# Out projection of a transformer block as three products of rounded halves, with the second norm computed row tile by row tile inside it

## Chip, cores, metric

One Trainium2 chip, one of its eight cores. The metric is device time in microseconds (us) of one execution; the median of the runs is compared.

## What is computed

Two transformer blocks follow each other on 256 tokens of 1024 channels, all in float32. The change lies at the end of the first block's mixer and in the norm behind it:

```
cat = concatenate([fourier(f), o_att, dn], axis=-1)      # 256 + 512 + 256 channels
x = x + g1 * (cat @ w_out)                               # w_out 1024 x 1024
h2 = rms(x, norm2) * (1 + sc2) + sh2                     # x*rsqrt(mean(x*x)+eps)*norm2
x = x + g2 * (square(relu(h2 @ w_ff1)) @ w_ff2)          # w_ff1 1024x4096, w_ff2 4096x1024
```

`dn` is the output of a gated delta rule in four heads, itself rms-normed per head and multiplied by a silu gate.

## The kernel before

Each engine has its own instruction stream, written by hand; the engines meet at semaphores. Tokens are in two row tiles t of 128, output channels in two halves hh of 512, contracted channels in eight groups k of 128. A list of jobs (`first_jobs`) gives every PSUM product a number, a bank and the engine that empties it; `w.open(name)` on TensorE waits until the bank's old job is emptied, `w.after(name)` until that job itself is, `r.open(name)` on a reader waits until the job is full. Banks 0 to 3 hold the four sums (t, hh) of the out projection.

Before the change, attention and the scan of the delta rule run in eight steps n; ScalarE copies transposed probabilities (`PT`), takes exponentials, and scales the products (`PV`). Behind step 7:

- TensorE transposes the attention output (`catA0`, `catA1`, line 2237), waits for `dn_ready`, transposes `dn` (`catD`, 2243), spreads the gate vectors g1 and g2 over all rows (`g0_*`, `g1_*`, line 2251, eight matmuls each, two records a matmul), and forms the out projection in float32 (line 2259, 32 matmuls of 512 columns, two records each). Eight matmuls on constants (`dense`, line 616) and a wait for `hat_ready` follow, then 16 transposes of the normed rows (`h2T0` to `h2T3`, 2269), `mlp_open` (line 693, four matmuls that open banks 0 to 3), and the MLP's loop (716, 718, 729).
- VectorE sums `dn` (2820, 2821), scales it with a factor that GpSimd raises to the power -0.5 (`power(5, ...)`, lines 2516 and 2519), and counts `dn_ready`. Then `add_gated(0)`: for each (t, hh) two instructions (2833, 2836) as the sum fills (`acc_full`); `split_low` (755); scale and shift of the transposed norm (2856); `split_y` (785).
- ScalarE copies the products out (2298), rounds the first MLP weights (`split_high`, 747), squares the two rows tile by tile (2486), waits for GpSimd's `power(6, ...)`, scales the rows (2493), and rounds the shifted channels (`y_high`, 2498).

The MLP already multiplies in halves: a number is the sum of a rounded part (high, a copy into the type fp32r on ScalarE) and the rest (low, a subtraction on VectorE), and a product is high*high + high*low + low*high. Weights come through a ring of four slots of 2 MB; `out0` and `out1` lie in slots 0 and 1, and the loads into these slots wait for `acc_full` 3 and 4. TensorE enters the MLP when `y_split` is 2 and `w_low` is 4.

## Time and profile before

| | us |
|---|---|
| three runs | 1560.35, 1561.5, 1569.91 (median 1561.5) |
| profiled execution, its own time | 1570.09 |
| its span, first to last instruction | 1568.3 |
| mean granted TensorE clock | 0.967 |

The profiled execution is 8.6 us above the median, and 1.8 us of its time lie outside its span. Times in the rows below are us from the span's start.

### The profile page before, as it was taken

To read this page: it belongs to the slowest core of one execution; us is meant where nothing else is said; L and a number is where in the kernel's file an instruction comes from. 1 tells how busy PE (TensorE), PEld (TensorE's weight loads), DVE (VectorE), ACT (ScalarE), POOL (GpSimd) and SP (SyncE) were. 2 spreads that over 40 slices of the span, in tenths; PEclk is the share of its full clock that TensorE was granted. 3 is DMA by queue.
4 is the path that set the end of the run, shared out by engine and by line. 5 is a ranking of instruction groups with operands and counts; after the bars stand their busy time and mean duration, and the time that the engine had idled before them with its cause. 6 is when DMAs were issued, how large, how long until landed. Compare 5 with 4: busy or idle time off the path is not lost. (4 is left out here: it accounts for less than half of the span.)

```text
span 1568.3 us, 25730 instructions
## 1 busy us (share of the span) xinstructions
PE 1472.4 (94%) x10597; PEld 1198.7 (76%) x10597; DVE 903.9 (58%) x1410; ACT 695.0 (44%) x1168; POOL 58.3 (4%) x73
## 2 busy tenths in 40 slices
PE   5999989988999989999899999998999989999996
PEld 2556767655888879898877888878989887788885
DVE  1653343425656556377586655575657768565655
ACT  3232325433444434376732444453547653344442
POOL 0000530000000000000000000000000000000000
PEclk9999999988999999999999999999999989999998
DMA  9630651006554426433237555524534223846420
GB/s 349 257 108 17 236 185 53 2 1 215 180 192 166 134 82 187 141 108 108 108 108 264 184 195 189 186 82 141 163 109 144 89 89 108 305 177 214 179 89 27
DMA packets 121038, 230.14 MB, mean 147 GB/s; under 512 B 20080, under 2 KB 34672, under 8 KB 120176
## 3 DMA queue, kind: packets, MB, share of 16 engines
q1 hardware_dynamic: 118064, 223.80, 41.0%
q10 hardware_dynamic: 2880, 5.01, 0.9%
q8 instruction: 68, 1.11, 0.3%
q14 instruction: 26, 0.21, 0.0%
HBM read 227.76 MB, written 1.05 MB: 146 GB/s over the span
## 5 line engine op out<-in xcount | busy, mean ns | idle before, releaser
L755 DVE TENSOR_TENSOR work_rounded<-ring,work_rounded 128x1024 fp32r<-128x1024 f32 x208 | 240.9, 1221 | 88.2 <-ACT work_rounded L747 88.1
L716 PE MATMUL psum<-channels_rounded,work_rounded 128*128 128x512 f32 x768 | 278.2, 405 | 0.0
L729 PE MATMUL psum<-work_rounded 128*128 128x512 f32 x1152 | 266.5, 390 | 0.0
L974 PE MATMUL psum<-channels_rounded,ring_rounded 128*128 128x256 f32 x1728 | 251.8, 288 | 2.8 <-PEq L2869 1.6
L747 ACT ACTIVATE work_rounded<-ring 128x1024 fp32r<-128x1024 f32 x208 | 203.2, 1049 | 106.4 <-PE psum L729 102.8
L729 PEld LDWEIGHTS psum<-work_rounded 128*128 128x128 f32 x1152 | 214.6, 188 | 45.5
L974 PEld LDWEIGHTS psum<-channels_rounded,ring_rounded 128*128 128x128 f32 x1728 | 225.6, 193 | 9.7 <-issue 8.8
L718 PE MATMUL psum<-channels_rounded,work_rounded 128*128 128x256 f32 x768 | 218.2, 284 | 0.0
L716 PEld LDWEIGHTS psum<-channels_rounded,work_rounded 128*128 128x128 f32 x768 | 147.3, 192 | 39.1 <-issue 2.5
L718 PEld LDWEIGHTS psum<-channels_rounded,work_rounded 128*128 128x128 f32 x768 | 148.1, 193 | 0.8
L1442 DVE TENSOR_TENSOR ring_rounded<-ring,ring_rounded 128x1024 fp32r<-128x1024 f32 x80 | 94.2, 1198 | 48.4 <-ACT ring_rounded L1246 47.8
L1246 ACT ACTIVATE ring_rounded<-ring 128x1024 fp32r<-128x1024 f32 x80 | 80.7, 1026 | 12.0 <-DMA ring<-in_w_in 12.0
L795 DVE TENSOR_TENSOR work<-work,psum 128x512 f32<-128x512 f32 x48 | 33.0, 688 | 86.8 <-ACT work L767 86.8
L767 ACT ACTIVATE work<-psum 128x512 f32<-128x512 f32 x48 | 28.7, 598 | 117.4 <-PE psum L718 117.4
L2298 ACT ACTIVATE work<-psum 128x512 f32<-128x512 f32 (+1 forms) x83 | 48.3, 582 | 57.7 <-PE psum L2014 32.0
L2014 PEld LDWEIGHTS psum<-work 64*64 64x64 f32 x1840 | 56.8, 136 | 17.2 <-issue 14.4
L974 PE MATMUL psum<-channels_rounded,work_rounded 128*128 128x256 f32 x384 | 69.0, 282 | 0.0
L2014 PE MATMUL psum<-work 64*64 64x64 f32 x1840 | 60.0, 221 | 7.9 <-issue 6.2
L1442 DVE TENSOR_TENSOR ring_rounded<-ring,work_rounded 128x1024 fp32r<-128x1024 f32 x46 | 54.0, 1220 | 19.0 <-ACT work_rounded L1246 19.0
L769 ACT ACTIVATE work_rounded<-work 128x512 fp32r<-128x512 f32 x48 | 30.4, 632 | 71.1 <-DVE work L797 71.1
L974 PEld LDWEIGHTS psum<-channels_rounded,work_rounded 128*128 128x128 f32 x384 | 58.8, 188 | 2.0 <-DVE ring_rounded L1442 0.7
L1246 ACT ACTIVATE work_rounded<-ring 128x1024 fp32r<-128x1024 f32 x46 | 45.2, 1051 | 29.2 <-DMA ring<-in_w_in 24.2
(366 smaller groups left out, 2018.5 us busy)
## 6 DMA issues: line engine op xcount, KB each, us to landing
ring<-in_w_in SPq DMA_DIRECT2D x20, 2048.0 KB, 8.3
ring<-in_w_ff SPq DMA_DIRECT2D x16, 2048.0 KB, 8.4
ring<-in_w_ff_in SPq DMA_DIRECT2D x16, 2048.0 KB, 7.7
ring<-in_w_ff_out SPq DMA_DIRECT2D x16, 2048.0 KB, 7.9
ring<-in_w_mod SPq DMA_DIRECT2D x12, 2048.0 KB, 8.9
ring<-in_w_out SPq DMA_DIRECT2D x6, 2048.0 KB, 7.8
ring<-in_w_in SPq DMA_DIRECT2D x8, 1024.0 KB, 5.7
ring<-in_w_up SPq DMA_DIRECT2D x4, 2048.0 KB, 7.9
```

The source lines that it names most:

```text
L716: pe.matmul(v3(psum[:, 4 + m, :], SEQ), w1[0][:, k, m * P:(m + 1) * P], y_both[:, :, k, :], start=(k == 0), stop=False, skip_group_check=True)
L718: mm = pe.matmul(psum[:, 4 + m, SEQ:512], w1[1][:, k, m * P:(m + 1) * P], y_both[:, 1, k, :], start=False, stop=(k == KC - 1), skip_group_ ...
L729: mm = pe.matmul(psum[:, 2 * t + n, :], h[ph][:, kq, t * P:(t + 1) * P], w2[pw][:, kq, n * 512:(n + 1) * 512], start=False, stop=False, sk ...
L747: act.activation(parts.high[i % 2][:, at], ring[:, SLOT * s + 1024 * c:SLOT * s + 1024 * (c + 1)], ACT.Copy).then_inc(w_high, 1)
L755: dve.tensor_tensor(parts.low[i % 2][:, at], ring[:, SLOT * s + 1024 * c:SLOT * s + 1024 * (c + 1)], exact(parts.high[i % 2][:, at]), ALU. ...
L769: act.activation(parts.h_high[:, 2 * q:2 * q + 2, :], parts.h[q], ACT.Copy).then_inc(hid_high, 1)
L795: dve.tensor_tensor(h, h, psum[:, 4 + 2 * q:6 + 2 * q, SEQ:512], ALU.add).then_inc(hid_sum, 1)
L974: mm = pe.matmul(ps[:, at:at + SEQ], u[pw][:, k, col:col + P], y_parts[py][:, k, :], start=((k, n) == (0, 0)), stop=((k, n) == (KC - 1, 2)))
L1246: act.activation(piece(high_of.get(name, high_slot), name, c), piece(raw(name), name, c), ACT.Copy).then_inc(piece_high, 1)
L1442: dve.tensor_tensor(piece(low_of(name), name, c), piece(raw(name), name, c), exact(piece(high_of.get(name, high_slot), name, c)), ALU.subt ...
L2014: mm = pe.matmul(ps[half(c), 256 * d + h * HD:256 * d + h * HD + HD], lhs[d][half(c), at], rhs[d][half(c), at], start=True, stop=True)
L2298: r.read(name, act.activation(dst, r.open(name, width), ACT.Copy))
```

## The change

The out projection takes its operands in halves. ScalarE rounds `w_out` in eight pieces of 128x1024 (`leaving_high`), seven of them inside the scan's steps and one behind; VectorE forms the low pieces in the ring's slots (`leaving_low`), and both halves of `cat` (`cat_rounded`, `cat_low`). TensorE makes 96 matmuls of 512 columns in fp32r in place of the 32 in float32: row tile 0 first, then row tile 1, with the transposes of row tile 0's norm between the halves of row tile 1. The gate rows g1 come ahead of `catD`, those for g2 behind the projection. Both powers go from GpSimd to ScalarE as logarithm and exponential. The norm goes row tile by row tile: ScalarE squares each half row as it arrives, ScalarE scales the left and VectorE the right half of a row, and the scale and shift are shared between both engines. `split_low` of the first MLP weights is cut in two pairs of pieces. The MLP's entry loses its wait for `h2T3` and keeps those for `y_split`.

```diff
-    for n in ("catA0", "catA1", "catD", "g0_0", "g0_1", "g1_0", "g1_1"):
-        j.add(n, "act")
-    for c in range(4):
-        j.add(f"h2T{c}", "dve")
+    for name, by, bank in (("catA0", "dve", 4), ("catA1", "dve", 5), ("g0_0", "act", 6), ("g0_1", "act", 7),
+                           ("catD", "dve", 3), ("h2T00", "dve", 4), ("h2T01", "act", 5), ("g1_0", "act", 6),
+                           ("g1_1", "act", 7), ("h2T10", "dve", 4), ("h2T11", "act", 5)):
...
-        def split_low(dve, units, parts, i, r=0):
-            for c in range(CHUNKS):
+            for c in chunks:
...
+            columns = lambda ap_at, n: work_rounded[:, ap_at:ap_at + n]
+            catT_at, akv_at = CB.shape[1], CB.shape[1] + 3072
+            cat_parts = [v3(columns(u_at + 5632, 2048), SEQ), v3(columns(catT_at, 2048), SEQ)]
+            out_high = [[xT_rounded[:, 1024 * c:1024 * (c + 1)] for c in range(4)],
+                        [columns(at, 1024) for at in (0, 1024, akv_at + 1024, akv_at)]]
...
+                    out_low = [rounded(q.slot(f"out{hh}"), 512) for hh in range(2)]
+
+                    def leaving(t, hh, k, wt, row, first=False, last=False):
+                        if wt == 0:
+                            weights = out_high[hh][k // 2][:, 512 * (k % 2):512 * (k % 2) + 512]
+                        else:
+                            weights = out_low[hh][:, k, :]
+                        mm = pe.matmul(psum[:, 2 * t + hh, :], cat_parts[row][:, k, t * P:(t + 1) * P], weights,
+                                       start=first, stop=last)
+                        if last:
+                            mm.then_inc(acc_full, 1)
+
+                    def normed(t, filled=0):
+                        for g, ready in enumerate((hat_left, hat_right)):
+                            ps = w.open(f"h2T{t}{g}")
+                            if g == 0:
+                                dense(pe, ps, filled)
+                            pe.wait_ge(ready, t + 1)
+                            for i in range(4):
+                                k = 4 * g + i
+                                mm = pe.transpose(ps[:, i * P:(i + 1) * P], v3(x_hat2, D)[:, t, k * P:(k + 1) * P],
+                                                  ident)
+                            w.done(mm)
+
+                    gate_rows_out(0)
                     ps = w.open("catD")
...
+                    pe.wait_ge(cat_high, 3)
+                    for k0, k1 in ((0, 6), (6, 8)):
+                        if k0:
+                            pe.wait_ge(cat_high, 4)
                         for hh in range(2):
+                            for k in range(k0, k1):
+                                pe.wait_ge(piece_high, 4 * hh + k // 2 + 1)
+                                leaving(0, hh, k, 0, 0, first=(k == 0))
+                    pe.wait_ge(cat_split, 1)
                     w.after("catD")
-                    for t in range(TT):
-                        for hh in range(2):
-                            u = landed(f"out{hh}")
-                            for k in range(KC):
-                                mm = pe.matmul(psum[:, 2 * t + hh, :], catT3[:, k, t * P:(t + 1) * P], u[:, k, :],
-                                               start=(k == 0), stop=(k == KC - 1))
-                            mm.then_inc(acc_full, 1)
-                    for c in range(4):
-                        ps = w.open(f"h2T{c}")
-                        if c == 0:
-                            dense(pe, ps, 8)
-                            pe.wait_ge(hat_ready, 3)
-                        for i in range(4):
-                            k, t = 2 * c + i // 2, i % 2
-                            mm = pe.transpose(ps[:, i * P:(i + 1) * P], v3(x_hat2, D)[:, t, k * P:(k + 1) * P], ident)
-                        w.done(mm)
-                    w.after("h2T3")
+                    for hh in range(2):
+                        for k in range(KC):
+                            leaving(0, hh, k, 0, 1)
+                    for hh in range(2):
+                        for k in range(KC):
+                            pe.wait_ge(piece_low, 4 * hh + k // 2 + 1)
+                            leaving(0, hh, k, 1, 0, last=(k == KC - 1))
+                    for hh in range(2):
+                        for k in range(KC):
+                            leaving(1, hh, k, 0, 0, first=(k == 0))
+                            leaving(1, hh, k, 0, 1)
+                            leaving(1, hh, k, 1, 0, last=(k == KC - 1))
+                        if hh == 0:
+                            normed(0)
+                    gate_rows_out(1)
+                    normed(1, 6)
...
+                    def leaving_high(hh, c):
+                        s = q.slot(f"out{hh}")
+                        act.wait_ge(unit_in[s], q.landed(f"out{hh}"))
+                        act.activation(out_high[hh][c], ring[:, SLOT * s + 1024 * c:SLOT * s + 1024 * (c + 1)],
+                                       ACT.Copy).then_inc(piece_high, 1)
...
+                        if n < 6:
+                            leaving_high(n // 4, n % 4)
+                        elif n == 7:
+                            leaving_high(1, 2)
...
+                    cat_rounded("catA0", 2)
+                    act.wait_ge(sums_ready, 5)
+                    step(act.activation(rs[:, 52:60], ss[:, 52:60], ACT.Ln, bias=eps, scale=1.0 / HD))
+                    step.wait()
+                    act.activation(rs[:, 52:60], rs[:, 52:60], ACT.Exp, scale=-0.5).then_inc(scales_ready, 1)
+                    cat_rounded("catA1", 4)
+                    act.activation(cat_parts[0][:, 0:2, :], catT3[:, 0:2, :], ACT.Copy).then_inc(cat_high, 1)
+                    leaving_high(1, 3)
+                    cat_rounded("catD", 6)
+                    gate_rows_in(0)
...
+                    def gathered(t, hh):
+                        act.wait_ge(x1_ready, 2 * t + hh + 1)
+                        step(act.activation(square_out[:, 0:512], x3[:, t, 512 * hh:512 * (hh + 1)], ACT.Square,
+                                            accum_out=ss[:, 60 + 2 * t + hh:61 + 2 * t + hh]))
+                        step.wait()
+                        one, arg = rs[:, 60 + t:61 + t], ln_arg[:, t:t + 1]
+                        if hh == 0:
+                            step(act.activation(arg, ss[:, 60 + 2 * t:61 + 2 * t], ACT.Identity, bias=eps,
+                                                scale=1.0 / D))
+                            return
+                        step(act.activation(one, ss[:, 61 + 2 * t:62 + 2 * t], ACT.Ln, bias=arg, scale=1.0 / D))
+                        step.wait()
+                        act.activation(one, one, ACT.Exp, scale=-0.5).then_inc(scales_ready, 1)
+                        act.wait_ge(scales_ready, 4 + t)
+                        act.mul(v3(x_hat2, D)[:, t, 0:512], x3[:, t, 0:512], one).then_inc(hat_left, 1)
+
+                    def normed(t):
+                        ps = r.open(f"h2T{t}1")
+                        for i in range(4):
+                            k = 4 + i
+                            last = act.activation(yT8[:, k, t * P:(t + 1) * P], ps[:, i * P:(i + 1) * P], ACT.Identity,
+                                                  bias=modT3[:, 24 + k, 0:1], scale=a2[:, k:k + 1])
+                            if i < 3:
+                                step(last)
+                        r.read(f"h2T{t}1", last)
+                        r.settle()
+                        for g in range(2):
+                            if g == 0:
+                                r.after(f"h2T{t}0")
+                            act.activation(quarter(y_high, t, g), quarter(half_T, t, g), ACT.Copy).then_inc(y_in, 1)
+
+                    gathered(0, 0)
+                    gathered(0, 1)
+                    gathered(1, 0)
+                    normed(0)
+                    gathered(1, 1)
+                    gate_rows_in(1)
+                    normed(1)
...
-                    power(5, 52, 8, 1.0 / HD)
-                    power(6, 60, 2, 1.0 / D)
...
+                    leaving_low(0, 0)
...
+                    cat_low("catA0", 2, 1)
+                    cat_low("catA1", 4, 2)
+                    dve.wait_ge(cat_high, 3)
+                    dve.tensor_tensor(cat_parts[1][:, 0:2, :], catT3[:, 0:2, :], exact(cat_parts[0][:, 0:2, :]),
+                                      ALU.subtract).then_inc(cat_split, 1)
+                    cat_low("catD", 6, 4)
+                    for c in range(1, 8):
+                        leaving_low(c // 4, c % 4)
...
+                    r.after("g0_1")
+                    gated(0, 0, 0, 1)
+                    gated(0, 0, 1, 2)
+                    scaled_right(0)
+                    split_low(dve, q, mlp, 0, chunks=(0, 1))
+                    gated(0, 1, 0, 3)
+                    shifted(0)
+                    step(low_quarter(0, 0))
+                    step(low_quarter(0, 1))
+                    split_low(dve, q, mlp, 0, chunks=(2, 3))
+                    gated(0, 1, 1, 4)
+                    scaled_right(1)
+                    shifted(1)
+                    r.settle()
+                    low_quarter(1, 0).then_inc(y_split, 2)
+                    low_quarter(1, 1).then_inc(y_split, 2)
```

`leaving_low` and `cat_low` are one subtraction each; `gated` has the two instructions of `add_gated`.

TensorE from the last attention transposes (first two rows of each: `catA1`) to the first products of the projection. Before:

```order
L2237 MATMUL psum<-shared_consts,work 128x128 [waits act_emptied]
L2237 MATMUL psum<-shared_consts,work 128x128 x3
L2243 MATMUL psum<-shared_consts,work 128x128 [waits dn_ready,act_emptied]
L2243 MATMUL psum<-shared_consts,work 128x128 x3
L2251 MATMUL psum<-shared_consts,small 128x128 [waits act_emptied]
```

After:

```order
L2245 MATMUL psum<-shared_consts,small 128x128 [waits act_emptied]
L2245 MATMUL psum<-shared_consts,small 128x128 x3
L2278 MATMUL psum<-shared_consts,work 128x128 [waits dn_ready,dve_emptied]
L2278 MATMUL psum<-shared_consts,work 128x128 x3
L2256 MATMUL psum<-channels_rounded,work_rounded 128x512 [waits piece_high,cat_high]
```

Half of the gate rows now stand ahead of the wait for `dn_ready`, and the projection directly behind it.

VectorE from the low parts to the MLP, after the change (2911: `cat`; 2905: `w_out`; 2934 and 2937: gate and add; 756: MLP weights):

```order
L2911 TENSOR_TENSOR work_rounded<-psum,work_rounded 128x512 [waits products_done,dve_emptied,cat_high]
L2905 TENSOR_TENSOR ring_rounded<-ring,channels_rounded 128x1024 [waits piece_high] x3
L2905 TENSOR_TENSOR ring_rounded<-ring,work_rounded 128x1024 [waits piece_high] x4
L2934 TENSOR_TENSOR work<-psum,work 128x512 [waits acc_full,act_emptied]
...
L756 TENSOR_TENSOR work_rounded<-ring,work_rounded 128x1024 [waits w_high] x2
L2934 TENSOR_TENSOR work<-psum,work 128x512 [waits acc_full]
L2937 TENSOR_TENSOR x_tok<-x_tok,work 128x512 [waits dve_step]
```

Before, the same stretch of VectorE held four pairs and then the MLP weights:

```order
L2825 TENSOR_TENSOR work<-work 128x512 [waits dve_step]
L2833 TENSOR_TENSOR work<-psum,work 128x512 [waits acc_full,act_emptied]
L2836 TENSOR_TENSOR x_tok<-x_tok,work 128x512 [waits dve_step]
...
L2836 TENSOR_TENSOR x_tok<-x_tok,work 128x512 [waits dve_step]
L755 TENSOR_TENSOR work_rounded<-ring,work_rounded 128x1024 [waits dve_step,w_high]
L755 TENSOR_TENSOR work_rounded<-ring,work_rounded 128x1024 [waits w_high] x3
```

Eleven subtractions now lie ahead of the first pair, and two pieces of MLP weights ahead of the last.

ScalarE in a step of the scan, before (2298: copy of `PT`; 2450: exponential; 2456: `PV`):

```order
L2298 ACTIVATE work<-psum 128x512 [waits products_done,act_emptied]
L2450 ACTIVATE work,small<-psum,small 128x512 [waits act_emptied,products_done,max_ready]
L2456 ACTIVATE work<-psum,small 128x64 [waits products_done,act_emptied,rden_ready]
L2298 ACTIVATE work<-psum 128x512 [waits products_done,act_emptied]
L2450 ACTIVATE work,small<-psum,small 128x512 [waits act_emptied,products_done,max_ready]
```

After (2332: copy of `PT`; 2484: exponential; 2495: `leaving_high`; 2490: `PV`):

```order
L2332 ACTIVATE work<-psum 128x512 [waits products_done,act_emptied]
L2484 ACTIVATE work,small<-psum,small 128x512 [waits act_emptied,products_done,max_ready]
L2495 ACTIVATE channels_rounded<-ring 128x1024 [waits unit_in0]
L2490 ACTIVATE work<-psum,small 128x64 [waits products_done,act_emptied,rden_ready]
L2332 ACTIVATE work<-psum 128x512 [waits products_done,act_emptied]
```

One rounding of a piece now stands between the exponential and the product behind it.

## Rows read from the trace of the kernel before

**Rows 1.** Windows of the span: busy time by engine, granted clock, DMA.

```profile
400.00:450.00 50.00, 50.00 (x257) 42.40 (x256) 31.47 (x32) 24.17 (x29) 0.00 (x0) 1.00 0.55 201
```

**Rows 2.** Timeline of TensorE: start, us, operation, idle before and releaser.

```profile
321.24 1.84 PE L2237 MATMUL psum<-shared_consts,work 128*128 128x128 f32 x8 [0.58 <-ACT work L2456]
325.50 1.09 PE L2243 MATMUL psum<-shared_consts,work 128*128 128x128 f32 x4 [2.42 <-DVE work L2825]
326.38 6.23 PE L2251 MATMUL psum<-shared_consts,small 128*128 128x128 f32 x32
332.45 27.63 PE L2259 MATMUL psum<-ring,work 128*128 128x512 f32 x64
359.92 5.32 PE L616 MATMUL psum<-shared_consts 128*128 128x384 f32 x16
368.08 2.70 PE L2269 MATMUL psum<-shared_consts,work 128*128 128x128 f32 x16 [2.84 <-ACT work L2493]
373.18 1.88 PE L693 MATMUL psum<-zeros 1*128 1x512 bf16 x4 [2.40 <-DVE xT L2856]
374.99 0.79 PE L716 MATMUL psum<-channels_rounded,work_rounded 128*128 128x512 f32 x1
```

**Rows 3.** Timeline of VectorE in the same stretch.

```profile
323.21 0.69 DVE L2823 TENSOR_TENSOR work<-work,small 128x512 f32<-128x512 f32 x1 [2.05 <-POOL small L2519]
339.59 0.69 DVE L2833 TENSOR_TENSOR work<-psum,work 128x512 f32<-128x512 f32 x1 [14.23 <-PE psum L2259]
361.75 4.63 DVE L755 TENSOR_TENSOR work_rounded<-ring,work_rounded 128x1024 fp32r<-128x1024 f32 x4
368.85 4.27 DVE L2856 TENSOR_SCALAR xT<-psum,small 128x256 f32<-128x256 f32 x8 [2.18 <-PE psum L2269]
373.03 2.49 DVE L785 TENSOR_TENSOR channels_rounded<-xT,channels_rounded 128x512 fp32r<-128x512 f32 x4
```

**Rows 4.** Timeline of ScalarE in the same stretch.

```profile
322.32 0.60 ACT L2298 ACTIVATE work<-psum 128x512 f32<-128x512 f32 x1 [1.23 <-PE psum L2237]
361.76 1.06 ACT L2486 ACTIVATE work<-x_tok 128x1024 f32<-128x1024 f32 x1 [12.64 <-DVEq L2838]
365.84 2.19 ACT L2493 ACTIVATE work<-x_tok,small 128x1024 f32<-128x1024 f32 x2 [2.93 <-POOL small L2519]
373.15 0.63 ACT L2498 ACTIVATE channels_rounded<-xT 128x512 fp32r<-128x512 f32 x1 [0.46 <-DVE xT L2856]
```

**Rows 5.** Timeline of TensorE, rounded matmuls of the MLP's second product.

```profile
388.36 11.11 PE L729 MATMUL psum<-work_rounded 128*128 128x512 f32 x48
399.31 0.39 PE L716 MATMUL psum<-channels_rounded,work_rounded 128*128 128x512 f32 x1
```

**Rows 6.** Windows: TensorE busy, then the others; third from last the granted clock.

```profile
331.50:332.00 0.50, 0.50 (x5) 0.50 (x5) 0.00 (x0) 0.19 (x1) 0.00 (x0) 0.90 0.00 0
369.00:370.00 1.00, 1.00 (x8) 1.00 (x7) 0.91 (x3) 0.12 (x1) 0.00 (x0) 0.57 0.93 332
379.00:380.00 1.00, 1.00 (x6) 0.87 (x6) 1.00 (x2) 0.09 (x1) 0.00 (x0) 0.81 0.00 0
```

**Rows 7.** Timeline of TensorE, MLP matmuls just behind its start.

```profile
375.79 0.63 PE L716 MATMUL psum<-channels_rounded,work_rounded 128*128 128x512 f32 x1
376.22 0.41 PE L718 MATMUL psum<-channels_rounded,work_rounded 128*128 128x256 f32 x1
```

**Rows 8.** Timeline of ScalarE, then of TensorE, in one step of the scan.

```profile
274.80 0.31 ACT L2456 ACTIVATE work<-psum,small 128x64 f32<-128x64 f32 x1
275.60 0.60 ACT L2298 ACTIVATE work<-psum 128x512 f32<-128x512 f32 x1 [0.49 <-PE psum L2166]
277.38 1.10 PE L2174 MATMUL psum<-work 128*128 128x64 f32 x8
```

**Rows 9.** ScalarE, groups by line: shapes, count, busy us, mean ns, idle.

```profile
L2331 ACT ACTIVATE xT<-psum,small 128x256 f32<-128x256 f32 x8 | 4.1, 560 | 2.0 <-DVEq L2586 1.9
L2380 ACT ACTIVATE small<-small 128x32 f32<-128x32 f32 x1 | 0.2, 233 | 0.0
```

128 lines of the change are left out of this document (60 added, 68 removed).

## Prediction

> **What bounds the kernel now.** I read the windows first, then the timelines of the three busy engines from the end of the scan to the MLP, then single rows for prices. In the MLP TensorE is busy for 50.00 us out of 50 at the full clock, with VectorE at 31 and ScalarE at 24 [rows 1]. So everything behind the MLP's first matmul moves with that matmul, and the change is worth what it shifts that matmul from 374.99 [rows 2]. Ahead of it the reader is to see a stretch of 53.75 us, from 321.24, in which TensorE has little parallel work and waits four times: 0.58, 2.42 (for `dn`), 2.84 (for the normed rows) and 2.40 us (for the last shift) [rows 2]. The 5.32 us of `dense` and the half of the gate rows that nobody needs there (3.1 of 6.23 us) are fill too. VectorE's 14.23 us of idle before its first gated sum [rows 3] and ScalarE's 12.64 [rows 4] show the room in which low parts can be formed. The norm is a serial tail: last sum full at about 360.1, squares at 361.76, then GpSimd, which ScalarE waits 2.93 us for, scaling to 368.03, eight shifts to 373.1, rounding and subtraction to 375.5 [rows 3, 4].
>
> **Rate of the projection.** Before: 64 records in 27.63 us, 0.86 us a float32 matmul [rows 2]. After: 96 rounded matmuls. The MLP's second product has the same form, 128x512 in fp32r: 48 of them between 388.36 and 399.31, 0.228 each [rows 5], so 21.9 us at the full clock, 5.7 less. At the lower clock, 1.2 GHz, one takes 0.43 (375.79 to 376.22) [rows 7].
>
> The Trainium skill (FP8 and Floating Point Precision, TensorE Precision Notes) says that a true FP32 product takes four passes through the array. By that three terms would cost 3/4 of 27.63, that is 20.7 us, and the sum would be 1.2 us better; the rows say 0.79 of it, and I go by the rows.
>
> **The scan.** ScalarE gets seven roundings of 128x1024 at about 1.05 (a square of that size takes 1.06 [rows 4]). Six stand in steps 0 to 5 between the exponential and `PV`. In the tightest step `PV` ends at 275.11, and ScalarE then waits 0.49 for the next transposes at 275.60 [rows 8]; a rounding ahead of it makes that copy 0.56 late, ending at 276.8 instead of 276.2. TensorE reads it at 277.38 [rows 8], 0.6 later still, so the cover holds and I take 0. If it does not, each step pays up to 0.56, and without any slack 1.05: 0 to 7.4 us. I take 0, since TensorE's row there has no idle before it: it is TensorE that sets the pace of a step.
>
> **The front, to the projection.** `catA` ends at 323.1 as before. The eight gate matmuls for g1 follow at once; their 16 records at the lower clock take 3.1 (half of 6.23 [rows 2]), to 326.2. On ScalarE the rounding of `catA0` (0.63) starts at 322.3, then logarithm and exponential of 0.23 each [rows 4, 9] end at 323.5. This replaces GpSimd, whose result VectorE took at 323.21 [rows 3]; VectorE has two small steps and one low piece (1.16) to do in between, which end at about 322.9. Its three steps of 0.73 so end at 325.75, 0.4 later than before, and hide under the gate rows. `catD` takes TensorE to 327.1 and the first product starts at 327.2, against 332.45. The gain there is the 2.42 of waiting, 3.1 of moved gate rows, less 0.4.
>
> **The projection and its low parts.** The clock in this execution was back at its upper level at 331.55 [rows 6], after TensorE had worked without a gap since 325.5. Now it works without a real gap from 321.24, so the clock could be back anywhere between 328 and 331.55. At the late end 10 matmuls run at 0.43 and the other 38 of row tile 0 at 0.228: sums 1 and 2 are full at 338.4 and 340.2. At the early end it is 1.6 us earlier. VectorE must have the low pieces ready by then: from 325.75 four subtractions of 512 columns (0.69 and the start, 2.9) to 328.8, then seven pieces at 1.16 (4.63 for four [rows 3]) to 336.9. The last piece is needed at 339.7 at the late end and at about 338.1 at the early one, so nothing waits, with 1 to 3 us to spare.
> Row tile 1, left half: 24 x 0.228 = 5.5, full at 345.7. The transposes of row tile 0 come next. Their input needs VectorE's two pairs (1.45 each, to 341.8), square, logarithm and exponential (0.8 + 0.5) and a scaling of 0.7: 344.0, so they don't wait and cost 8 x 0.15 = 1.2. Right half: 346.9 to 352.4. The queue loads into slots 0 and 1 wait for sums 3 and 4, which come 7 us earlier than now (sum 3 filled after three quarters of 27.63, at 353.2), so the transfers are no later relative to the MLP.
>
> **The tail.** Here the order on VectorE decides. After two low pieces of MLP weights (to 346.0) it takes the third pair to 347.5, shifts to 348.7, waits for ScalarE (square 0.8, four shifts from PSUM, rounding 0.63: 350.95), subtracts twice to 352.4, then does two more pieces of weights to 354.7, although the last sum was full at 352.4. That queue costs 2.3 us of the tail. Last pair to 356.2; square, logarithm, exponential to 357.6; scaling to 358.3. TensorE covers this with the other gate rows (16 records at the full clock, 1.7) and six `dense` (6/8 of 5.32, 4.0), to 358.1, then transposes to 359.5. ScalarE copies the two gate rows (1.25, to 359.6), shifts four times, rounds (362.0), and VectorE subtracts a quarter: 362.8. The shift of 128x128 with scale and bias is in no row. It lies between 0.23 (a row of 32 columns) and 0.56 (256 columns) [rows 9]; four cost 0.9 to 2.2, I take 1.7, from the middle, since it is half of the wider size. VectorE's lies between 0.27 and 0.53 (half and all of 4.27/8 [rows 3]); I take 0.3. The MLP starts at 362.9 at the late end of the clock and at 361.3 at the early end.
>
> **Sum.** 374.99 - 362.9 = 12.1, or 13.7. I take the middle, 13 us. The late end is made of 5.2 at the front (332.45 to 327.2), 5.7 from the rate and 4.4 from the tail behind the last sum (14.9, from 360.1 to 375.0, against 10.5), less 1.2 of transposes and 2.0 of low clock (10 x 0.2) inside the projection. Against the profiled execution's 1570.09 that is 1557; against the median of 1561.5, which lies 8.6 lower, **1548.5**. The unknown prices move it by +-1.5, the clock by +-0.8, hence 1546 to 1551.5 for this case.
>
> **The MLP's start** is the doubtful place for the clock. Before, it stood at the lower level from 369 until 379 [rows 6], and 4.2 us of MLP ran at half rate, which lost 2.1. After the change TensorE is idle for about 2 us ahead of the MLP, so I expect nearly the same loss and take 0 for the difference.
>
> **Rivals.**
> 1. The clock stays up. TensorE's gap ahead of 369 was 2.84 us [rows 2], now the only one is of about 2, behind the four matmuls of `mlp_open`. If the clock does not fall and also returns early in the projection, the gain is 13.7 + 2.1, 15.8, or 1545.5. For it speaks that the projection now leads into the tail with gate rows, `dense` and transposes without a gap; against it, that 2 us are not much less than the 2.84 behind which the clock fell.
> The clock's fall at 369 came during transposes, 0.57 in that window [rows 6]. The Trainium skill (TensorE: Matmul & The Clock Gate, Part 4: PE-mode transpose) says that transposes do not count as a busy array for the clock; by that `catD` interrupts the busy stretch at the front too, and the late end, 12.1, is the right one.
> 2. The cover is thin on ScalarE or VectorE: steps of the scan stretch, or the low pieces come late, since eleven subtractions stand ahead of the first pair. Price 2.2 (four steps at 0.56) up to 7.4; with 5 the time is 1553.5. Against it: the slack above.
> 3. The norm is not hidden, so the change does not do what it says: the tail stays as long as it was because of the queue on VectorE and ScalarE's added work. Then only the rate is left, 5.7: 1555.8.
> 4. Slower than before: the projection's matmuls, fed from the ring and the old `cat`, run at 0.43 and not at 0.228, because small waits for `piece_low` hold the clock at its lower level throughout. 96 x 0.43 = 41.3, 19.4 more: +6.4, 1568. It decides from 0.36 us a matmul (0.228 + 13/96). Against it: there is no wait in the last two thirds, and the clock came back within 6 us of steady work.
>
> **Chances.** Forecast 0.48, rival 1 0.22, rival 2 0.18, rival 3 0.08, rival 4 0.04. A change of 1%, 15.6 us, is about what a measurement of this kernel can tell from none (its three runs span 9.6 us). Faster by more than 1% is most of rival 1 and an edge of the forecast, 0.27; within 1% 0.70; slower by more than 1% needs rival 4 with something on top, 0.03. The range runs from rival 1 with the unknown prices at their good ends (1544) and 3 us for the spread of a median, a third of those 9.6, to rival 3 and the worse half of rival 2 with 2 us more: 1541 to 1558.
>
> **What would show it.** After: the first fp32r product near 327 and the MLP's first matmul at 361 to 363; no idle time of TensorE in the 96 matmuls above 0.3 us; `catA1` done on TensorE at 323.1, so no step of the scan longer; VectorE's last pair starting when the second pair of weight pieces ends. The prediction is wrong if `catA1` ends later than 323.4, if a low piece is waited for, or if ScalarE's shifts cost 0.56 each and push the MLP past 364.

## The result and the profile after

The changed kernel takes **1551.9 us** (median of five runs, 1547.1 to 1554.2), the kernel before 1561.6 (1560.4 to 1569.9) beside it: a ratio of 0.992 (0.989 to 0.995), 9.7 us. In a second set of runs it took 1549.3 against 1565.4, 0.9895 (0.9877 to 0.9914), 16.1 us. The forecast was 1548.5, in 1541 to 1558. Its profiled execution has a span of 1552.0 us, the one of before 1568.3.

TensorE in the stretch, by the timeline of the changed kernel:

```profile
323.11 1.91 PE L2237 MATMUL psum<-shared_consts,work 128*128 128x128 f32 x8 [0.58 <-ACT work L2490]
324.82 2.79 PE L2245 MATMUL psum<-shared_consts,small 128*128 128x128 f32 x16
327.56 0.63 PE L2278 MATMUL psum<-shared_consts,work 128*128 128x128 f32 x4
327.94 1.63 PE L2256 MATMUL psum<-channels_rounded,work_rounded 128*128 128x512 f32 x6
...
335.38 3.89 PE L2256 MATMUL psum<-ring_rounded,work_rounded 128*128 128x512 f32 x16
...
344.63 1.03 PE L2269 MATMUL psum<-shared_consts,work 128*128 128x128 f32 x8
...
351.06 1.95 PE L2245 MATMUL psum<-shared_consts,small 128*128 128x128 f32 x16
352.84 4.04 PE L617 MATMUL psum<-shared_consts 128*128 128x384 f32 x12
356.71 1.07 PE L2269 MATMUL psum<-shared_consts,work 128*128 128x128 f32 x8
357.71 1.03 PE L694 MATMUL psum<-zeros 1*128 1x512 bf16 x4
361.31 0.79 PE L717 MATMUL psum<-channels_rounded,work_rounded 128*128 128x512 f32 x1 [2.56 <-DVE channels_rounded L2956]
```

I call **the stretch** what lies between the start of `catA`'s transposes and the MLP's first matmul. It was 321.24 to 374.99, 53.75 us [rows 2], and is now 323.11 to 361.31, 38.20. Of TensorE's four waits of before, the 0.58 ahead of `catA` is unchanged, and the three inside the stretch are one: the first product starts 4.83 behind `catA` (before 11.21), 96 matmuls and eight transposes run without a gap from 327.94 to 351.06, and the only idle time, 2.56, is ahead of the MLP. The last sum is full at 351.06, so the tail, from there to the MLP, is 10.25 us; it was 15. In a second execution of the same kernel the clock was up at the front, TensorE passed the gate rows faster, and it then waited 1.17 us for `dn`:

```profile
327.71 0.63 PE L2278 MATMUL psum<-shared_consts,work 128*128 128x128 f32 x4 [1.17 <-DVE work L2921]
```

`catD` starts 4.01 behind `catA` there, against 4.26 in the kernel before and 4.45 above, so at the front the wait for `dn` is covered by the gate rows and not gone.

VectorE around the last two sums, by its timeline (L2934 opens a gated pair, L756 are pieces of MLP weights):

```profile
349.67 1.29 DVE L2956 TENSOR_TENSOR channels_rounded<-xT,channels_rounded 128x512 fp32r<-128x512 f32 x2 [1.96 <-ACT channels_rounded L2571]
350.88 2.35 DVE L756 TENSOR_TENSOR work_rounded<-ring,work_rounded 128x1024 fp32r<-128x1024 f32 x2
353.15 0.68 DVE L2934 TENSOR_TENSOR work<-psum,work 128x512 f32<-128x512 f32 x1
```

The sum is full at 351.06 and its pair starts at 353.15: the two pieces of weights in between hold it up by 2.1 us. ScalarE's added work in the tail, two copies and four shifts:

```profile
356.54 1.21 ACT L2332 ACTIVATE work<-psum 128x512 f32<-128x512 f32 x2
357.88 1.50 ACT L2562 ACTIVATE xT<-psum,small 128x128 f32<-128x128 f32 x4
359.46 1.15 ACT L2571 ACTIVATE channels_rounded<-xT 128x512 fp32r<-128x512 f32 x2
```

The windows of the changed kernel at the front and at the MLP's start (third from last the granted clock) answer to [rows 6]:

```profile
324.00:326.00 2.00, 2.00 (x11) 2.00 (x10) 1.27 (x3) 1.76 (x5) 0.00 (x0) 0.50 0.00 0
326.00:327.00 1.00, 1.00 (x9) 1.00 (x9) 0.97 (x2) 1.00 (x2) 0.00 (x0) 0.72 0.00 0
327.00:331.00 4.00, 4.00 (x23) 3.36 (x22) 3.91 (x6) 2.93 (x6) 0.00 (x0) 1.00 0.00 0
...
360.00:361.00 1.00, 0.00 (x0) 0.00 (x0) 0.78 (x2) 1.00 (x3) 0.00 (x0) 0.85 1.06 397
361.00:367.00 6.00, 5.69 (x17) 4.86 (x18) 5.15 (x5) 3.41 (x4) 0.00 (x0) 0.50 0.46 166
```

The clock is back at 2.4 GHz before 327, ahead of the first product, and falls during the idle 2.56 us, about 0.6 us before the MLP starts. The MLP's first 6 us run at 1.2 GHz.

**Where the rest of the time is.** The span cut at the same four instructions in every kernel (us; "end" is the first block's end, from the first transposes of the new tokens to the second block's first product):

```
                 to catA  stretch   MLP      end    block 2   span
before           321.2    53.75    182.69   12.47   998.2    1568.3
before, again    318.7    53.56    182.41   12.43   994.8    1561.9
after            323.1    38.20    183.38    9.93   997.4    1552.0
after, again     323.7    37.61    183.35    9.92   995.6    1550.2
```

The stretch gives 15.4 to 16.1 us, more than the forecast's 13; the end gives another 2.5; the MLP loses 0.7 to 0.9. Ahead of `catA`, where the programs differ only by the roundings in the scan, and in block 2, where they are the same, two executions of one kernel differ by 0.6 to 3.4 us in each part (6.4 in the whole span of the kernel before), together with the clock: the changed kernel's runs had spans of 1552.0, 1552.3, 1549.4, 1550.0 and 1545.2 at a mean granted clock of 0.967, 0.967, 0.969, 0.972 and 0.976. That is why two sets of runs of one pair of kernels say 9.7 and 16.1. The stretch can be read to 0.6 us, the median to 3 or 4 (1561.6 to 1565.4 for the kernel before in four sets of runs).

### The profile page after: what moved, and what is told of

Same layout as the page of the kernel before. It is cut to its first block and busy times, and to the rows that moved or that the text cites. A ratio compares the mean times of both kernels' runs of the same rounds, so it can differ in the third digit from the quotient of the medians.

```text
span 1552.0 us, 25832 instructions
## 1 busy us (share of the span) xinstructions
PE 1461.4 (94%) x10625; PEld 1203.5 (78%) x10625; DVE 916.3 (59%) x1424; ACT 707.4 (46%) x1197; POOL 54.5 (4%) x69
## 5 line engine op out<-in xcount | busy, mean ns | idle before, releaser
L756 DVE TENSOR_TENSOR work_rounded<-ring,work_rounded 128x1024 fp32r<-128x1024 f32 x208 | 241.0, 1221 | 86.5 <-ACT work_rounded L748 86.5
```

What stands on the lines that cost most here:

```text
L756: dve.tensor_tensor(parts.low[i % 2][:, at], ring[:, SLOT * s + 1024 * c:SLOT * s + 1024 * (c + 1)], exact(parts.high[i % 2][:, at]), ALU. ...
```

## The experiments

All are measured by the stretch first, then by the time. Twelve kernels ran, four on each of three chips, those of one chip against the same runs of the kernel before (median 1565.4 for the first four rows; 1564.9 for two terms, float32 projection, norm row behind and gate rows in one; 1563.8 for the other four).

```
                       stretch   time (median)   ratio to before
before, again          53.56     1563.7 (one)
after, again           37.61     1549.3          0.9895 (0.9877 to 0.9914)
dense ahead of MLP     37.93     1548.4          0.9896 (0.9879 to 0.9913)
weights later          36.02     1545.3          0.9887 (0.9867 to 0.9907)
two terms              38.40     1549.1          0.9902 (0.9880 to 0.9924)
float32 projection     44.03     1553.4          0.9934 (0.9908 to 0.9960)
norm row behind        39.85     1549.1          0.9903 (0.9880 to 0.9927)
norm behind, no dense  37.35     1549.8          0.9914 (0.9895 to 0.9934)
gate rows in one       39.95     1551.1          0.9904 (0.9883 to 0.9926)
gate rows last         36.03     1544.5          0.9869 (0.9844 to 0.9893)
powers alone           50.42     1562.1          0.9983 (0.9968 to 0.9999)
end alone              52.51     1569.5 (one)
```

**Both kernels again.** No edit. The stretch of the kernel before came out 0.2 shorter, that of the changed kernel 0.6 shorter.

> The kernel before, unchanged, profiled once more. Question: how much of the difference between two executions lies outside the changed stretch. The stretch is from the first catA1/catA0 transpose to the MLP's first matmul: 53.75 us in the first profile of before, 38.20 in that of after, so 15.55 less, while the medians differ by 9.7. Theory A (the clock's phase): the granted clock stands low at other times in this execution, the stretch comes out 1 to 5 us shorter than 53.75 (the gate rows or the MLP's start then run at the full clock), and the mean clock is above 0.967 if the time is below 1570. Theory B (the stretch is as long as before and the changed kernel loses 5 to 6 us elsewhere): the stretch is 53.7 again within 0.5, and the part behind the MLP's first matmul is 1188 us or less.

> The changed kernel, unchanged, on the same chip as the three beside it, as their reference. Theory A: its stretch is between 38 and 41 us depending on when the clock returns in the projection; time 1547 to 1555, its profile's mean clock and its time go together. Theory B: the part behind the MLP's first matmul is again 1190 us or more whatever the clock.

The stretch repeats, so the gain of 15.4 to 16.1 is the change's and not an accident of the clock in one execution. The view that the changed kernel loses 5 to 6 us somewhere else falls too: with the same programs in a second set of runs the medians were 16.1 apart. What varied is time outside the stretch. (Behind the MLP's first matmul both kernels took about the same: 1193.3 and 1189.6 us before, 1190.7 and 1188.9 after.)

**`dense` ahead of the MLP.** Four `dense` matmuls behind `mlp_open`, in a bank whose old job TensorE first waits to see emptied (that wait is not among the lines shown):

```diff
             mlp_open(pe)
+            if filled:
+                dense(pe, psum[:, 7, :], filled)
```

> The changed kernel with four more matmuls on constants behind mlp_open, 2.6 us of fill in the 2.56 us in which TensorE waits for the first rounded channels; they compute nothing that is used. Theory 1 (the clock falls at the MLP's start because of that idle time, and costs about 2.6 to 3 us, 6.3 us of MLP at half rate): the clock stays at its upper level through the MLP's start, the first 16 products there run at 0.35 us a pair and not 0.64, and the kernel is about 2.5 us faster than a_again. Rival (the clock falls because of the low activity ahead of it, transposes and one-row matmuls, and a fill of this kind does not prevent it): the clock falls all the same and the time is a_again's within 1 us, or up to 0.5 us worse where the fill ends after the channels are ready.

The window of this kernel at the MLP's start:

```profile
360.00:366.00 6.00, 6.00 (x34) 5.00 (x33) 5.37 (x6) 3.63 (x4) 0.00 (x0) 1.00 0.50 185
```

34 records in 6 us at the full clock against 17 at half (the window 361 to 367 above). The MLP took 180.90 instead of 183.35: the half clock at its start costs 2.5 us. That the fill is what kept the clock up is likely but not shown by one profile, since the next kernel kept it up too, with a gap of 2.41 us and no fill. The median, 0.9 lower than beside it, is too coarse to show either.

**The weights later.** VectorE takes the last gated pair first, and then the second pair of weight pieces, one on each side of its scaling; three `dense` instead of six:

```diff
-                    split_low(dve, q, mlp, 0, chunks=(2, 3))
                     gated(0, 1, 1, 4)
+                    split_low(dve, q, mlp, 0, chunks=(2,))
                     scaled_right(1)
+                    split_low(dve, q, mlp, 0, chunks=(3,))
                     shifted(1)
```

> The changed kernel with VectorE's second pair of MLP weight pieces moved behind the last gated sum (one piece before the scaling, one behind), and three dense matmuls in place of six ahead of the last transposes. In the profile of after the last sum is full at 351.1 and VectorE takes it at 353.15. Theory of the prediction (that queue costs 2 us of the tail): last gated pair starts 2 us earlier, and with half of the dense gone the transposes and the MLP's first matmul come 1.9 us earlier: stretch 36.3, time 2 us less. Rival (the tail is covered elsewhere, by MLP weight pieces that the MLP's entry waits for, or the clock falls earlier because of the missing dense matmuls): the first matmul moves by less than 0.7 us, or moves by 2 and the time stays, since the MLP then starts at half rate for longer.

VectorE, then TensorE, in this kernel:

```profile
347.54 0.69 DVE L2934 TENSOR_TENSOR work<-psum,work 128x512 f32<-128x512 f32 x1 [0.29 <-PE psum L2256]
...
347.34 1.95 PE L2245 MATMUL psum<-shared_consts,small 128*128 128x128 f32 x16
355.55 0.50 PE L717 MATMUL psum<-channels_rounded,work_rounded 128*128 128x512 f32 x1 [2.41 <-DVE channels_rounded L2956]
```

Now VectorE waits for the sum (0.29) and not the sum for VectorE. The tail is 8.2 instead of 10.25, the stretch 36.02, 1.6 to 2.2 shorter: the forecast's queue, measured, together with the three `dense` that had to go with it so that the transposes could come earlier; the two were not tried apart. The clock did not fall at the MLP here, though TensorE was idle for 2.41 us.

**Two terms.** The product of `cat`'s low part with the weights' high part is left out (32 matmuls; both low parts are still formed):

```diff
-                            leaving(0, hh, k, 0, 1)
...
-                            leaving(1, hh, k, 0, 1)
```

> The changed kernel without one of the three terms: the product of the low part of `cat` with the high part of the weights is left out (its low part is still formed), so the output is less exact and TensorE has 32 matmuls of 0.228 us, 7.3 us, less to do in the projection. The measure is the stretch from the start of the `catA` transposes to the MLP's first matmul, 37.6 to 38.2 us in the changed kernel and 53.6 to 53.8 in the kernel before. Theory A, the rate: TensorE sets the length of the projection and the tail hangs on the last sum, so the stretch gets shorter by 7.3, to 30.6, and the time by the same. Theory B, the queue on VectorE: the low parts of the weights end at 337.9 whatever TensorE does, so row tile 0 gains only 0.9 (337.9 and two matmuls, against 339.2), TensorE then waits for `piece_low`, and behind it pair, weight pieces, pair, shifts, quarters, weight pieces and pair stand on VectorE without a gap; the last sum is full 4 to 5 us earlier but its pair starts only 0.9 earlier. The stretch gets shorter by 0.9 to 1.5, to about 37, and what TensorE saved stands as idle time ahead of the tail's transposes.

TensorE, then VectorE:

```profile
328.75 0.73 PE L2256 MATMUL psum<-ring_rounded,work_rounded 128*128 128x512 f32 x2 [0.19 <-DVE ring_rounded L2901]
...
342.83 1.95 PE L2245 MATMUL psum<-shared_consts,small 128*128 128x128 f32 x16
351.89 1.97 PE L2269 MATMUL psum<-shared_consts,work 128*128 128x128 f32 x8 [3.24 <-ACT work L2552]
...
348.36 0.68 DVE L2930 TENSOR_TENSOR work<-psum,work 128x512 f32<-128x512 f32 x1
```

Theory B holds in its mechanism. With 7.3 us less for TensorE the stretch is no shorter, 38.40. TensorE waits for low pieces, still fills the last sum 24.0 us behind `catA` instead of 27.95, and then stands idle, since VectorE comes to the pair 29.53 behind `catA` instead of 30.04. During the idle 3.24 us the clock falls, and the transposes run at half clock, which the forecast of B, 0.9 to 1.5 shorter, did not have. **From about here VectorE's chain sets the end of the stretch**; TensorE's rate has nothing more to give.

**The projection in float32.** The changed kernel's order with the old 32 float32 matmuls, without the roundings and low parts of the two:

```diff
-                                leaving(0, hh, k, 0, 0, first=(k == 0))
...
+                                mm = pe.matmul(psum[:, 2 * t + hh, :], catT3[:, k, t * P:(t + 1) * P], u[:, k, :],
+                                               start=(k == 0), stop=(k == KC - 1))
```

> The changed kernel's order of work with the old 32 matmuls in float32 from `cat` and the ring, and without the high and low pieces of the two: only the rounding is undone, the norm by row tiles, the moved gate rows and ScalarE's powers stay. The measure is the stretch from the start of the `catA` transposes to the MLP's first matmul, 37.6 to 38.2 us in the changed kernel and 53.6 to 53.8 before. Theory A, the rate is worth what the forecast said: the projection takes 27.6 instead of 23.1 minus 1.0 of transposes, so the last sum is full 5.5 us later and the stretch is 5.5 longer, 43.5. Theory B, VectorE's queue swallows part of it: the pair of weight pieces that stands ahead of the last gated pair is done while the sum is still filling, so the 2.1 us of queue vanish and the stretch is 3.4 longer, about 41.4. Either way it stays 10 us or more below the kernel before, and that part belongs to the reordering and not to the three terms.

```profile
323.76 20.87 PE L2285 MATMUL psum<-ring,work 128*128 128x512 f32 x48 [0.75 <-ACT work L2318]
...
345.34 7.03 PE L2285 MATMUL psum<-ring,work 128*128 128x512 f32 x16
352.20 1.95 PE L2245 MATMUL psum<-shared_consts,small 128*128 128x128 f32 x16
353.99 4.04 PE L617 MATMUL psum<-shared_consts 128*128 128x384 f32 x12
357.86 1.04 PE L2269 MATMUL psum<-shared_consts,work 128*128 128x128 f32 x8
```

Theory A by its result: 44.03, 5.8 to 6.4 longer. The projection takes 5.3 more (323.76 to 352.20 against 327.94 to 351.06) and starts 0.7 later behind `catA` than in the first execution of the changed kernel (1.1 later than in the second, which had the full clock at the front as this one has), behind ScalarE's copy of `catD`. Half of B holds, the pair starts 0.7 behind the full sum (VectorE at 352.92) and not 2.1; but the `dense` matmuls also start later and keep the transposes to 357.86, with their input there at 356.4. So the three terms, with the forming of their halves, are worth 6 of the 16 us, and the new order with float32 throughout, powers included, the other 9.6.

**The norm row behind the projection.** On all three engines the work on row tile 0 follows the last sum, and VectorE takes the second pair of weight pieces while that sum fills (of the edit, TensorE's part):

```diff
-                        if hh == 0:
-                            normed(0)
+                    normed(0)
                     gate_rows_out(1)
                     normed(1, 6)
```

> The changed kernel with the transposes, shifts, roundings and low quarters of row tile 0 moved behind the whole projection, on all three engines; VectorE takes its second pair of weight pieces while the last sum fills. Only the hiding of the norm row inside the projection is undone. The measure is the stretch, 37.6 to 38.2 us in the changed kernel. Theory A, the hiding is what shortened the tail: behind the last sum now come four transposes and four shifts more on each of two engines, two roundings and two quarters, 1.5 + 1.15 us on ScalarE and as much on VectorE, so the tail of 10.25 grows to 13 or more, less 1.0 of transposes that leave the projection: the stretch is 2 to 4 us longer. Theory B, the hiding is worth nothing because the queue it makes on VectorE (2.1 us ahead of the last pair) costs as much: the last sum is full 1.0 earlier, the pair starts at once, ScalarE's added 2.65 us follow its scaling, and the stretch changes by less than 0.7.

```profile
351.04 4.14 PE L617 MATMUL psum<-shared_consts 128*128 128x384 f32 x12 [2.04 <-DVE xT L2947]
355.01 1.03 PE L2269 MATMUL psum<-shared_consts,work 128*128 128x128 f32 x8
```

39.85, 1.65 to 2.2 longer, at the lower end of theory A. But the reason is in these rows: the `dense` matmuls wait for the bank until 351.04 and then keep the transposes back to 355.01, while their input was there at 349.9. So the same again without `dense`:

```diff
-                    normed(1, 6)
+                    normed(1, 0)
```

> The kernel with the whole norm row behind the projection, now without the six `dense` ahead of the transposes of row tile 1. There they stood behind a wait for the bank that VectorE's shifts free (351.04), took 4.0 us, and kept the transposes waiting to 355.01 although their input was ready at about 349.8; the stretch was 39.85. Theory A, that hiding the norm row inside the projection shortens the tail: the stretch stays 1.5 us or more above the changed kernel's 37.6 to 38.2. Theory B, that TensorE's fill made the loss and the hiding itself is worth little as long as VectorE's weight pieces stand ahead of the last gated pair: the transposes start at +31.5 behind the start of `catA`, ScalarE's two gate copies end at +34.0, four shifts, a rounding and a quarter follow, and the MLP starts at about +37.0; it then starts at half clock, since TensorE idles some 4 us ahead of it, and loses up to 2.5 us there.

```profile
346.68 0.69 DVE L2933 TENSOR_TENSOR work<-psum,work 128x512 f32<-128x512 f32 x1 [1.64 <-PE psum L2256]
...
351.35 1.16 PE L2269 MATMUL psum<-shared_consts,work 128*128 128x128 f32 x8 [2.04 <-DVE xT L2947]
...
357.22 0.79 PE L717 MATMUL psum<-channels_rounded,work_rounded 128*128 128x512 f32 x1 [2.90 <-DVE channels_rounded L2955]
```

37.35: theory B. The last sum is full at 346.49 and its pair starts at 346.68: the queue on VectorE is gone, and what it had cost, 2.1 us, pays for the norm of row tile 0 in the tail. Hidden inside the projection or not, that norm makes no difference to the stretch here. The six `dense` behind the bank's wait had cost 2.5 us of the stretch. In the time nothing of this shows: the MLP begins at half clock and takes 183.05 instead of 182.09, and the ratios of the two kernels, 0.9903 and 0.9914, cannot be told apart.

**The gate rows in one wait.** All sixteen gate matmuls and their copies before row tile 0 is done, none in the tail:

```diff
+                    gate_rows_out(1)
                     for hh in range(2):
                         for k in range(KC):
                             leaving(0, hh, k, 0, 1)
...
-                    gate_rows_out(1)
```

> The changed kernel with the second wait of gate rows undone: all 16 gate matmuls and their copies stand ahead of or in the middle of row tile 0's products, as one group, and none in the tail. The measure is the stretch, 37.6 to 38.2 us in the changed kernel. Theory A: TensorE's 1.95 us of gate rows now lie in the projection and delay the last sum by as much, and the tail, which hangs on VectorE's pair and ScalarE's norm and not on the gate rows that fill TensorE's waiting, gives back at most the 1.2 us of ScalarE's copies: the stretch changes by +0.8 to +1.9. Theory B, the last sum is not what the tail waits for but VectorE's second pair of weight pieces (queue 2.1 us): then 1.95 us more in the projection are swallowed by that queue, and the copies that leave the tail make the stretch 0 to 1.2 us shorter, though TensorE idles longer ahead of the MLP and may start it at half clock, which costs up to 2 us behind the stretch.

```profile
351.61 0.68 DVE L2934 TENSOR_TENSOR work<-psum,work 128x512 f32<-128x512 f32 x1
...
355.14 1.09 PE L2269 MATMUL psum<-shared_consts,work 128*128 128x128 f32 x8 [1.87 <-ACT work L2557]
```

39.95, 1.75 to 2.3 longer: theory A, a little beyond its end. Every pair of VectorE starts later with its sum, the last 32.0 us behind `catA` instead of 30.04, so the queue swallows nothing, and ScalarE's two copies that leave the tail give nothing back, since the shifts wait for the transposes (1.18 us idle ahead of them).

**The gate rows last.** The weights later, as above, and the second gate rows behind the transposes of row tile 1 on TensorE and ScalarE, with the six `dense` ahead of these transposes again; TensorE waits for the copies inside the MLP, where it first writes that bank:

```diff
-                    gate_rows_out(1)
-                    normed(1, 3)
+                    normed(1, 6)
+                    gate_rows_out(1)
```

> The changed kernel with both cures for its tail. VectorE's second pair of weight pieces stands behind the last gated pair, as in the run that had that alone (stretch 36.02). And the second gate rows stand behind the transposes of row tile 1 instead of ahead of them, on TensorE and ScalarE, with six `dense` ahead of these transposes: so TensorE has 1.8 us of matmuls in the gap ahead of the MLP, and ScalarE's shifts need not wait for its two copies (1.21 us). TensorE waits for these copies in the MLP only where it first writes the third bank. If ScalarE's copies are on the path, its shifts start when the transposes end, 0.8 us earlier than in that run, and the stretch is 35.2; if TensorE's fill is what the transposes wait for, it stays at 36.0 or grows to 36.5. If the clock stays up at the MLP's start as it did there, the stage from the MLP's first matmul to the next transposes takes 180.5 to 181, otherwise up to 183.4. The time should be 0.986 to 0.988 of the kernel before.

```profile
346.87 4.04 PE L617 MATMUL psum<-shared_consts 128*128 128x384 f32 x12
350.74 1.04 PE L2271 MATMUL psum<-shared_consts,work 128*128 128x128 f32 x8
351.61 1.95 PE L2247 MATMUL psum<-shared_consts,small 128*128 128x128 f32 x16
...
355.09 0.49 PE L719 MATMUL psum<-channels_rounded,work_rounded 128*128 128x512 f32 x1 [0.56 <-DVE channels_rounded L2958]
```

The gap ahead of the MLP is 0.56 us of TensorE's instead of 2.4, the clock stays up (1.00 from 355 to 361; the MLP takes 180.52), and the stretch is 36.03, as with the weights alone: there ScalarE's shifts waited for its copies, here for the transposes behind six `dense`, and they start 32.75 us behind `catA` in both. At 1544.5 us, 0.9869, this is the fastest kernel here; of 36.02 and 1545.3 it cannot be told apart.

**The powers alone**, in the kernel before: logarithm and exponential on ScalarE for GpSimd's two powers.

```diff
+                    step(act.activation(rs[:, 52:60], ss[:, 52:60], ACT.Ln, bias=eps, scale=1.0 / HD))
+                    step.wait()
+                    act.activation(rs[:, 52:60], rs[:, 52:60], ACT.Exp, scale=-0.5).then_inc(scales_ready, 1)
...
-                    power(5, 52, 8, 1.0 / HD)
-                    power(6, 60, 2, 1.0 / D)
```

> The kernel before with one part of the change alone: the two powers (of the eight head sums ahead of `dn`, and of the two norm sums) are logarithm and exponential on ScalarE instead of GpSimd's. The forecast put 2.42 us of waiting for `dn` on it at the front, and the tail had 2.93 us in which ScalarE waited for GpSimd, for which two steps of 0.2 to 0.3 now stand. If both are on the path, the first product comes 1.2 to 2.4 us earlier behind the start of `catA` (11.0 to 11.2 in the kernel before) and the stretch of 53.6 to 53.8 gets shorter by 3.5 to 4.5; if ScalarE's added steps delay its copies of `catA`, the front gains less than 1.2.

VectorE at the front, then TensorE and ScalarE in the tail:

```profile
319.49 0.69 DVE L2826 TENSOR_TENSOR work<-work,small 128x512 f32<-128x512 f32 x1 [1.86 <-ACT small L2480]
...
355.62 5.32 PE L616 MATMUL psum<-shared_consts 128*128 128x384 f32 x16
361.45 1.97 PE L2269 MATMUL psum<-shared_consts,work 128*128 128x128 f32 x16 [0.51 <-ACT work L2498]
368.12 0.79 PE L716 MATMUL psum<-channels_rounded,work_rounded 128*128 128x512 f32 x1 [0.34 <-DVE channels_rounded L785]
...
359.21 2.19 ACT L2498 ACTIVATE work<-x_tok,small 128x1024 f32<-128x1024 f32 x2
```

In the tail the two steps are worth 2.6 us (last sum to MLP 12.5 instead of 15.1; 2.3 of it lie ahead of the transposes, and the rest behind them, where this execution had the full clock and the others half of it). At the front they are worth 0.2: VectorE waits 1.86 for ScalarE where it waited 2.05 for GpSimd [rows 3]. The stretch is 3.1 to 3.3 shorter; what is over the 2.8 lies in gate rows at the full clock. The median is 1.7 lower.

**The end alone**, in the kernel before: the gated additions count `x_next` up themselves.

```diff
-                            if g == 1:
-                                dve.sem_inc(x_next, 1)
+                            if g == 1:
+                                dve.tensor_tensor(xs, xs, out_tmp, ALU.add).then_inc(x_next, 1)
+                                dve.wait_ge(x_next, i + 1)
```

> The kernel before with the end of the first block as the changed kernel has it: the second gated sums count x_next up by the addition itself and not by an instruction of their own. Nothing was forecast of this. Four pairs of VectorE start every 1.57 us in the kernel before and every 1.45 in the changed one, so 0.5 us are expected from it. The stage from the first transposes of this end to the second block's first matmul was 12.45 in the kernel before and 9.93 or 11.61 in the changed kernels. If the counting explains it, the stage is 10 to 11.6 here; if the clock explains the rest, it is about 12 and the difference between 9.93 and 11.61 goes with the place of the half clock, at the first two groups of transposes or at the last two.

VectorE there, first pairs, in the kernel before again and then in this one:

```profile
553.13 0.69 DVE L2833 TENSOR_TENSOR work<-psum,work 128x512 f32<-128x512 f32 x1 [3.58 <-PE psum L736]
...
554.70 0.69 DVE L2833 TENSOR_TENSOR work<-psum,work 128x512 f32<-128x512 f32 x1 [0.15 <-DVE x_tok L2836]
```

```profile
556.06 0.69 DVE L2833 TENSOR_TENSOR work<-psum,work 128x512 f32<-128x512 f32 x1 [3.58 <-PE psum L736]
...
557.51 0.69 DVE L2833 TENSOR_TENSOR work<-psum,work 128x512 f32<-128x512 f32 x1
```

A pair every 1.45 us instead of 1.57, and the end is 11.95, 0.5 shorter: that much of the 2.5 is the counting. In four kernels with the changed code (weights later, two terms, norm behind, gate rows last) the end took 11.60 or 11.61, in the other six 9.92 to 9.95. In all four the half clock lay from 5.7 or 6.0 to 9.2 or 9.4 us behind the start of the end, on the last transposes; in all six it had passed by 3.8 us. So 1.7 of the 2.5 go with where the half clock lay; it was not tried by itself. The last 0.3 is the difference between 11.95 and 11.61 at about the same place of the half clock. It stands as idle time of TensorE just ahead of the second block's first product, 1.56 us here and in the kernel before and 1.21 in the changed one; why is open. This execution also had the clock up earlier at the front, with the front as it was before: the first product came 9.94 behind `catA` and not 11.21. So up to 1.3 us of what [rows 2] show ahead of the projection belong to the clock of that execution.

## Why the prediction was right, and where not

**Right in sign, size and cause of most of it**; the forecast of 1548.5 is 3.4 below one median and, by the ratio of the second set, 3.4 above (0.9895 of 1561.5 is 1545.1). What the change does to the stretch itself was forecast at 40.1 to 41.7 us and came out at 37.6 to 38.2.

- *The rate*, "5.7 less": 96 matmuls and eight transposes took 23.12 us; the transposes take 0.79 of it (344.63 to 345.42), so the matmuls took 22.3, 0.233 each and not 0.228. The run in float32 put 5.3 us on the projection and 5.8 to 6.4 on the stretch. The row of the MLP was the better price. The Trainium skill's four passes (FP8 and Floating Point Precision, TensorE Precision Notes) would have made it 20.7.
- *The scan*, 0: from the first `PT` transposes (260.70 in the changed kernel) to `catA` it is 62.39 to 62.42 us in all fourteen profiles, with seven roundings or none. In the step of [rows 8] (below) the copy is 0.3 late and not 0.56; everything is 1.87 later in that execution, and 275.60 has become 277.76. Nothing behind it moves. By its letter one sign of being wrong came true, "if `catA1` ends later than 323.4": `catA`'s transposes ended at 325.0. But the length from the scan's last steps to `catA` is unchanged, and over the fourteen profiles `catA` starts anywhere from 317.7 to 323.7, in either kernel. The sign should have been a length and not a time from the start of the span. The marks "near 327" and "at 361 to 363" were met (327.94, 361.31) by the same luck: behind `catA` both came earlier than forecast, the second by 1.9 us or more.
- *The front*, "327.2, against 332.45", that is 5.96 behind `catA`: it was 4.83, in others 4.4. The gate rows took 2.8 us and not 3.1 and `catD` 0.4 ahead of the product and not 0.9; both ran partly or wholly at the full clock. `dn` was 0.2 earlier and not 0.4 later, and with the clock up it was waited for again, 1.17 us, which the prediction had at nothing.
- *The clock in the projection*, between a late end (-2.0) and an early one (-0.4): **this step was mis-sized.** It was back before 327 and the first rounded matmul, so none of the ten or so products forecast at 0.43 us ran at half rate, and the projection took 23.1 us where the late end had 25.2 and the early one 23.6. It came back some 2 us into the gate rows, between the transposes of `catA` and `catD`; in all ten profiles with the changed order it was up when the first product started. By the Trainium skill (TensorE: Matmul & The Clock Gate, Part 4: PE-mode transpose) the late end was to be the right one; no run here bears that out.
- *The low pieces*: "to 336.9", 15.7 behind `catA`: they ended at 337.9, 14.8 behind it, and no matmul waited.
- *The tail*, 10.5: 10.25. The queue on VectorE, "2.3": 2.1, and 1.6 to 2.2 in the run that took it away. Four shifts of ScalarE, 1.7: 1.50, from 0.38 each.
- *The MLP's start*, "nearly the same loss": 6.2 us at half clock instead of 4.4 (the prediction read 4.2), 0.7 us more. Right in kind.
- *Not seen*: the end of the first block, -2.5 in the profile, of which 0.5 is the counting and 1.7 goes with the clock. I had read `add_gated` for its place in the norm row and not for its second use.
- *The step to the median* took 8.6 off the profiled execution. The profile of before was a long one (1570.1 us against medians of 1561.6 to 1565.4), the one of after was 1.9 above its median. The sum in the profiles was 16.3 us, not 13; it came near the median partly by luck, because that step and the terms that were sized too small (clock, front, end) went opposite ways. Rival 1's time has a slip in it: 1561.5 less 15.8 is 1545.7, not 1545.5.

ScalarE in that step of the scan, after:

```profile
276.48 1.05 ACT L2495 ACTIVATE channels_rounded<-ring 128x1024 fp32r<-128x1024 f32 x1
277.43 0.30 ACT L2490 ACTIVATE work<-psum,small 128x64 f32<-128x64 f32 x1
277.76 0.60 ACT L2332 ACTIVATE work<-psum 128x512 f32<-128x512 f32 x1
```

Of the rivals, a clock that stays up at the MLP (rival 1) did not come in this kernel but does in three others, for 2.5 to 2.9 us. Its other half, an early return of the clock in the projection, did come. The second, a thin cover, and the fourth, products at 0.43 us throughout, are answered above: no step of the scan is longer, and no product waited or ran at half rate. The third, that the norm row is not really hidden, was right about its mechanism: queue and gain cancel. It was wrong about its price, since the tail is shorter for other reasons: the powers (2.6 in the kernel before) and, for the other 2.2, by my reading the norm taken by halves, 512 columns behind the last sum instead of 1024; the halves were not tried alone.

## What to carry to other kernels

Where one engine fills its waits with work for later, put that work behind the step that somebody waits for and not ahead: two pieces of weights on VectorE ahead of the last gated pair cost 2.1 us of the stretch, all that hiding a norm row had gained. When an engine gets faster, look at once whose chain is now the longest; a third less of TensorE's work in this projection gave nothing. And fill an idle engine only with work that cannot stand in the way of its next real instruction: four us of `dense` behind a wait for a bank cost 2.5 of the stretch, though no median showed it.

## What was not expected of the hardware

- Where TensorE's clock is low is not fixed by the order of instructions. In the stretch the kernel before was at 1.2 GHz for 16 us in both its executions, and with the same code up to the MLP for 10.7 in another (the run of the end alone); the changed kernel for 4.0 and 0.7. The first products behind `catA` move by 1.3 us with it.
- At the MLP's start TensorE had been idle for 2.56 us and ran its first 6 us at half clock, and so it did in the second execution, behind 2.41; in the kernel with the weights later it had also been idle for 2.41 and the clock stayed at 1.00. In the float32 kernel, again behind 2.41, it fell only when the MLP had run for 1.5 us. So the length of the gap alone does not decide it in these runs. With 0.56 idle, or `dense` in the gap, it stayed up in both cases that were run.
- An instruction of VectorE's that only counts a semaphore up, between two dependent additions, costs 0.12 us.
- The same two steps of ScalarE for a power of GpSimd's are worth 0.2 us at the front and 2.6 in the tail. At the front VectorE makes the sums and takes the result, and ScalarE's logarithm stands behind its copy of `catA0`: VectorE waits 1.86 us instead of 2.05. In the tail ScalarE makes the sums and scales itself, nothing crosses to another engine, and 0.6 us stand for a wait of 2.93 [rows 4].
